# Query blocks filled ahead of the small steps, turned values copied by two engines, keys times beta formed ahead of the decays

## The reference, cut to what matters

```
x = x + 1/2 * RMSNorm(SwiGLU_1(RMSNorm(x)))
x = x + RMSNorm(Mix(RMSNorm(x)))
x = x + 1/2 * RMSNorm(SwiGLU_2(RMSNorm(x)))
```

```
# sample attention: scores of the new token's queries with all cached keys
s = einsum('bqhd,bkhd->bhqk', q, k) / 8 + cq - ck
# delta rule over the prompt, in chunks of 64 tokens
gc    = cumsum(g);  decay = exp(gc_i - gc_j) below the diagonal
kb    = k * beta
lower = (kb @ k.T) * decay;   attn = (q @ k.T) * decay
rhs   = [v * beta, kb * exp(gc)];  k_left = k * exp(g_last - gc)
```

## Time and profile before

| | |
|---|---|
| median of 3 runs | 1599.41 us (1598.86 to 1602.84) |
| profiled execution, its own time | 1597.58 us |
| its span, first to last instruction | 1595.3 us |
| PE busy | 1506.3 us, 94% of the span |
| DVE busy | 627.2 us, 39% |
| ACT busy | 500.7 us, 31% |
| POOL busy | 224.2 us, 14% |
| mean granted clock | 0.975 |
| DMA | 268.77 MB, mean 168 GB/s |

### The profile page before, as it was taken

How to read it: one execution, slowest core, us unless ns; L and a number is a source line. 1 busy time by engine, 2 the same in 40 slices (tenths; PEclk the granted TensorE clock), 3 DMA queues, 4 the chain that set the end, 5 groups by cost and what they waited for, 6 DMA issues and landing times. The chain is left out here.

```text
span 1595.3 us, 31169 instructions
## 1 busy us (share of the span) xinstructions
PE 1506.3 (94%) x12556; PEld 1382.2 (87%) x12556; DVE 627.2 (39%) x929; ACT 500.7 (31%) x740; POOL 224.2 (14%) x204
## 2 busy tenths in 40 slices
PE   7999999999688999999988999979979999999995
PEld 7999999999577888877866887759979999999995
DVE  4434343111633664133447443346253333432223
ACT  5322223211521355221124323242343222222221
POOL 0111111000252000323100220011031111110000
PEclk9999999999899999999989999989989999999998
DMA  4222222221449987999976757936212222223221
GB/s 151 92 92 92 92 92 99 92 90 62 146 149 387 340 299 249 366 336 341 377 260 217 238 186 259 300 116 227 80 40 90 86 89 90 92 97 109 81 83 53
DMA packets 111939, 268.77 MB, mean 168 GB/s; under 512 B 15401, under 2 KB 15914, under 8 KB 111090
## 3 DMA queue, kind: packets, MB, share of 16 engines
q1 hardware_dynamic: 105586, 244.25, 44.6%
q0 software_dynamic: 6272, 23.34, 4.0%
HBM read 253.29 MB, written 14.26 MB: 168 GB/s over the span
## 5 line engine op out<-in xcount | busy, mean ns | idle before, releaser
L131 DVE TENSOR_TENSOR w_low<-w_raw,w_high 128x1024 fp32r<-128x1024 f32 (+1 forms) x180 | 233.2, 1297 | 648.9 <-ACT w_high L127 648.8
L127 ACT ACTIVATE w_high<-w_raw 128x1024 fp32r<-128x1024 f32 (+1 forms) x180 | 200.7, 1116 | 731.6 <-PE psum L152 691.9
L148 PE MATMUL psum<-h_high,w_high 128*128 128x260 f32 x1344 | 270.5, 282 | 1.7 <-DVE w_low L131 1.7
L152 PE MATMUL psum<-h_high,w_low 128*128 128x260 f32 x1344 | 270.9, 283 | 0.0
L150 PE MATMUL psum<-h_low,w_high 128*128 128x260 f32 x1344 | 270.4, 283 | 0.0
L148 PEld LDWEIGHTS psum<-h_high,w_high 128*128 128x128 f32 x1344 | 207.2, 188 | 2.4 <-DVE w_low L131 2.4
L152 PEld LDWEIGHTS psum<-h_high,w_low 128*128 128x128 f32 x1344 | 207.2, 188 | 0.0
L150 PEld LDWEIGHTS psum<-h_low,w_high 128*128 128x128 f32 x1344 | 206.6, 188 | 0.0
L148 PE MATMUL psum<-mix_h_high,w_high 128*128 128x260 f32 x704 | 147.6, 291 | 6.3 <-DVE mix_h_low L296 6.1
L148 PE MATMUL psum<-a_high,w_high 128*128 128x260 f32 x704 | 144.2, 286 | 0.0
L150 PE MATMUL psum<-mix_h_low,w_high 128*128 128x260 f32 x704 | 142.5, 284 | 0.0
(11 more groups left out here) (324 smaller groups left out, 1921.3 us busy)
## 6 DMA issues: line engine op xcount, KB each, us to landing
kv_ring<-in_cache_k SPq DMA_DIRECT2D x256, 256.0 KB, 4.5
kv_ring<-in_cache_v SPq DMA_DIRECT2D x256, 256.0 KB, 4.4
w_raw<-in_w_gu SPq DMA_DIRECT2D x88, 512.0 KB, 3.2
w_raw<-in_w_dn SPq DMA_DIRECT2D x32, 704.0 KB, 4.0
w_raw<-in_w_proj SPq DMA_DIRECT2D x44, 512.0 KB, 6.7
spill<-h_f POOLq DMA_DIRECT2D x20, 260.0 KB, 5.2
gates<-spill POOLq DMA_DIRECT2D x16, 260.0 KB, 3.9
w_raw<-in_w_merge SPq DMA_DIRECT2D x8, 512.0 KB, 4.4
```

The source lines that it names most:

```text
L127: act.activation(w_high[:, u, 0:nk, :], w_raw[:, u, 0:nk, :], ACT.Copy).then_inc(high_done, 1)
L131: dve.tensor_tensor(w_low[:, u, 0:nk, :], w_raw[:, u, 0:nk, :], w_high[:, u, 0:nk, :].bitcast(F32), ALU.subtract).then_inc(low_done, 1)
L148: pe.matmul(out[h], w_high[:, u, k, :], high[:, k0 + j, tok[h]], start=s, stop=False)
L152: mm = pe.matmul(out[h], w_low[:, u, k, :], high[:, k0 + j, tok[h]], start=False, stop=e)
```

## The change

It has three parts; no arithmetic is added or taken out.

1. On DVE `queries(0)` moves from behind the small steps to ahead of them, behind a wait for `lin_out` (the copy of block 3 by ACT). `split_low` of block 6 moves from behind the scan to ahead of the reciprocal.
2. Of the four copies of turned values ACT does banks 0 and 1 (new semaphore `vt_first`), DVE banks 2 and 3. On DVE they now stand ahead of the low parts of g and beta. PE waits for both semaphores.
3. In `spread` DVE forms KB and v times beta first, with no wait but `p_bc`, and then waits for exp(g). The count of `p_dve` changes: KB is 1, v is 2, the difference is 3, KBE 4. In `raw` PE waits for count 2 alone ahead of k times KB, which now goes to bank 7 (beta's bank, read by then), and for the decays only ahead of k times q.

```diff
@@ scalar, before the attention loop
                     act.activation(gbr[64:68, 1, :], cum[64:68, :], ACT.Copy).then_inc(parts_high, 1)
+                    act.wait_ge(stored, 48)
+                    act.wait_ge(vt_pe, NQ)
+                    for b in range(NQ // 2):
+                        act.activation(vtok[:, b, :], psum[:, b, :], ACT.Copy).then_inc(vt_first, 1)
                     act.wait_ge(levels_in, 32)
@@ scalar, spread
-                            act.wait_ge(p_dve, 9 * i + 1)
+                            act.wait_ge(p_dve, 9 * i + 3)
                             act.activation(el[:, :], el[:, :], ACT.Exp).then_inc(p_act, 1)
@@ vector, small steps
                     split_low(dve, n0 + 5, 1, KD)
+                    dve.wait_ge(lin_out, Q0 + 4)
+                    queries(0)
                     dve.wait_ge(small_act, 5)
...
                     dve.tensor_scalar(rows[0:64, :], wsum[0:64, :], coef[0:64, 0:1], -1.0, ALU.mult,
                                       ALU.mult).then_inc(small_dve, 1)
+                    split_low(dve, n0 + 6, 0, KD)
                     dve.wait_ge(small_dve, 5)
                     dve.reciprocal(rows[64:96, :], wb[64:96, :]).then_inc(small_dve, 1)
...
-                    dve.wait_ge(lin_out, Q0 + 4)
-                    queries(0)
                     for n in range(4, NB):
-                        if n + 2 < NB:
+                        if 4 < n < NB - 2:
                             split_low(dve, n0 + 2 + n, n % 2, KD)
@@ vector, before the attention loop
                     queries_apart(0)
+                    dve.wait_ge(stored, 48)
+                    dve.wait_ge(vt_pe, NQ)
+                    for b in range(NQ // 2, NQ):
+                        dve.tensor_copy(vtok[:, b, :], psum[:, b, :]).then_inc(vt_copy, 1)
                     dve.wait_ge(parts_high, 1)
...
-                    dve.wait_ge(stored, 48)
-                    dve.wait_ge(vt_pe, NQ)
-                    for b in range(NQ):
-                        dve.tensor_copy(vtok[:, b, :], psum[:, b, :]).then_inc(vt_copy, 1)
@@ vector, spread
+                            dve.tensor_tensor(tmp[:, KB, :], k, psum[:, 7, :], ALU.mult).then_inc(p_dve, 1)
+                            dve.tensor_tensor(v, v, psum[:, 7, :], ALU.mult).then_inc(p_dve, 1)
                             dve.wait_ge(p_act, 3 * i + 1)
+                            dve.tensor_copy(gl[:, :], gb[:, :, C - 1]).then_inc(p_last, 1)
                             dve.tensor_copy(egl[:, i, :], ...).then_inc(p_last, 1)
-                            dve.tensor_copy(gl[:, :], gb[:, :, C - 1]).then_inc(p_last, 1)
-                            dve.wait_ge(p_last, 2 * i + 2)
+                            dve.wait_ge(p_last, 2 * i + 1)
                             dve.tensor_tensor(el[:, :]..., gb, ALU.subtract).then_inc(p_dve, 1)
-                            dve.tensor_tensor(v, v, psum[:, 7, :], ALU.mult).then_inc(p_dve, 1)
-                            dve.tensor_tensor(tmp[:, KB, :], k, psum[:, 7, :], ALU.mult).then_inc(p_dve, 1)
-                            dve.wait_ge(p_dve, 9 * i + 3)
+                            dve.wait_ge(p_dve, 9 * i + 1)
                             dve.tensor_tensor(tmp[:, KBE, :], tmp[:, KB, :], eg[:, :], ALU.mult).then_inc(p_dve, 1)
@@ vector, raw
-                            dve.tensor_tensor(lt[:, i, :], psum[:, 5, :], tmp[:, DT, :], ALU.mult).then_inc(p_dve, 1)
+                            dve.tensor_tensor(lt[:, i, :], psum[:, 7, :], tmp[:, DT, :], ALU.mult).then_inc(p_dve, 1)
@@ tensor (twice: key_pair with r, and after the transposes)
-                    pe.wait_ge(vt_copy, NQ)
+                    pe.wait_ge(vt_first, NQ // 2)
+                    pe.wait_ge(vt_copy, NQ // 2)
@@ tensor, raw
-                            pe.wait_ge(p_dve, 9 * i + 3)
-                            pe.wait_ge(p_act, 3 * i + 2)
+                            pe.wait_ge(p_dve, 9 * i + 2)
                             k = cv[:, 4 + i, 0:SEQ]
                             for p in range(NQ):
-                                pe.matmul(pr(psum[:, 5, :], p), pr(k, p), pr(tmp[:, KB, :], p), start=True, stop=True)
+                                pe.matmul(pr(psum[:, 7, :], p), pr(k, p), pr(tmp[:, KB, :], p), start=True, stop=True)
+                            pe.wait_ge(p_act, 3 * i + 2)
                             for p in range(NQ):
                                 mm = pe.matmul(pr(psum[:, 6, :], p), pr(k, p), pr(cv[:, i, 0:SEQ], p), start=True, stop=True)
```

More of the change, by code:

```diff
@@ L670, in core @@
             vt_copy = sem("fox_values_copied")
+            vt_first = sem("fox_first_values_copied")
             fs_pe = sem("fox_scores")
@@ L1271, in _ @@
                     split_low(dve, n0 + 5, 1, KD)
-                    dve.wait_ge(small_act, 5)
-                    dve.scalar_tensor_tensor(out=wsum[:, :], in0=wz[:, :], scalar=0.0, in1=wl[:, :],
-                                             op0=ALU.max, op1=ALU.add).then_inc(small_dve, 1)
-                    dve.tensor_scalar(wb[64:96, :], wb[64:96, :], 1.0, None, ALU.add).then_inc(small_dve, 1)
-                    dve.wait_ge(small_dve, 4)
-                    dve.tensor_scalar(rows[0:64, :], wsum[0:64, :], coef[0:64, 0:1], -1.0, ALU.mult,
-                                      ALU.mult).then_inc(small_dve, 1)
-                    dve.wait_ge(small_dve, 5)
-                    dve.reciprocal(rows[64:96, :], wb[64:96, :]).then_inc(small_dve, 1)
-                    dve.wait_ge(small_dve, 7)
-                    dve.tensor_tensor_scan(cum[:, :], starts[:, :], rows[:, 0:SEQ], 0.0, ALU.mult,
-                                           ALU.add).then_inc(small_dve, 1)
                     def queries(r):
@@ L1295, in queries @@
                                                 ).then_inc(qbd_done, 1)
+                    dve.wait_ge(lin_out, Q0 + 4)
+                    queries(0)
+                    dve.wait_ge(small_act, 5)
+                    dve.scalar_tensor_tensor(out=wsum[:, :], in0=wz[:, :], scalar=0.0, in1=wl[:, :],
+                                             op0=ALU.max, op1=ALU.add).then_inc(small_dve, 1)
+                    dve.tensor_scalar(wb[64:96, :], wb[64:96, :], 1.0, None, ALU.add).then_inc(small_dve, 1)
+                    dve.wait_ge(small_dve, 4)
+                    dve.tensor_scalar(rows[0:64, :], wsum[0:64, :], coef[0:64, 0:1], -1.0, ALU.mult,
+                                      ALU.mult).then_inc(small_dve, 1)
+                    split_low(dve, n0 + 6, 0, KD)
+                    dve.wait_ge(small_dve, 5)
+                    dve.reciprocal(rows[64:96, :], wb[64:96, :]).then_inc(small_dve, 1)
+                    dve.wait_ge(small_dve, 7)
+                    dve.tensor_tensor_scan(cum[:, :], starts[:, :], rows[:, 0:SEQ], 0.0, ALU.mult,
+                                           ALU.add).then_inc(small_dve, 1)
                     def new_forgets():
```

## The result

The change takes the median from 1601.07 us (1597.81 to 1603.62, six runs) to 1583.80 (1580.31 to 1584.70, six runs): a ratio of 0.9889, 95% interval [0.9874, 0.9904], 17.3 us. The forecast was 1582.0. The profiled execution took 1584.02.

A forecast was written before the change was run, and what follows sets the result against it. PE, busy for 94% of the span, was taken as the bound, so time could come only from its idle or low-clock places. 8.6 + 2.5 + 4.7 + 1.5 = 17.3 us gave 1582 against the median, range 1578 to 1588.

The forecast's parts named there:

- The queries: Between block 4 and the first key pair: PE's 6.98 us wait and 1.59 of low clock go, 8.6 us together.
- The turned values: Before the first scores: copies on ACT and DVE side by side let PE resume 2.5 us earlier.
- KB first: At `raw` of the four heads: PE's waits for KB shrink, 4.7 us in sum, ends 4 to 5.4.
- what is late next: At `turn` 2: PE still waits for DVE's list, so 1.0 of head 2's 1.5 us was counted.
- The clock: Three low-clock stretches from 818 to 861 us: 1.5 us gained net, ends 3.6 and -1.5.
- the second stretch: Low clock from 824 to 831 us, priced at some 1.4 us: should go.
- the first may: Low clock from 818 to 824 us, priced at some 2.7 us: may go, half counted.
- the third likely stays: Low clock from 854 to 861 us, priced at some 2.8 us: likely stays in some form.
- transfers did not eat part 1: Rival, key waits between 480 and 600 us: they grow from 6.1 to 12.2, gain 11.2, time 1588; chance 0.06.
- the copies were held by the gathers: Rival at the queries: one copy passes per gather, the pair starts as before, gain 8.7, time 1591; chance 0.03.
- the clock was not low for long: Rival: clock at 0.50 from 816 to 867 us, 12 us slower, time 1611; chance 0.02.

The follow-up runs named there:

- before_again: The kernel before the change, with no edit, run and profiled a second time on the first chip: 1601.0 us (one run).
- Part 1 alone: Kernel before plus only the early query copies and the early `split_low` of block 6: 1590.07 us, ratio to before 0.9937.
- part 2 alone: Kernel before plus only the turned-value copies shared by ACT and DVE, ahead of the low parts: 1597.30 us, ratio to before 0.9970.
- part 3 alone: Kernel before plus only KB and v formed first, PE waiting for these alone, KB's product into bank 7: 1596.10 us, ratio to before 0.9972.
- q_last: Changed kernel, with DVE's product of q with its decay moved behind the attention matrix: 1573.98 us, ratio to before 0.9863.
- after_again: Changed kernel with no edit, profiled once on the second chip: 1574.87 us (one run).
- bank0_first: Changed kernel, but PE starts the scores after ACT's first copy and waits for the other banks later: 1575.56 us, ratio to before 0.9883.
- ring_late: Changed kernel, with the third and fourth slot of the first keys loaded later, behind two more weight blocks: 1575.85 us, ratio to before 0.9886.
- after_timed: Changed kernel with no edit, timed on the third chip: 1577.01 us, ratio to before 0.9885.
- split_late: Changed kernel, with `split_low` of block 6 back at its old place behind the scan: 1576.89 us, ratio to before 0.9882.

## Why the prediction was right, point by point

The stages by lead, second profile of before less the changed kernel's, both with the stretch of single matmuls (start times in us):

| place | before_again | changed | lead | gained since the row above |
|---|---|---|---|---|
| first key pair | 476.08 | 467.30 | 8.8 | 8.8 |
| second key pair | 485.31 | 475.12 | 10.2 | 1.4 |
| last pair of the projection | 816.62 | 806.50 | 10.1 | -0.1 |
| first scores | 825.69 | 813.12 | 12.6 | 2.5 |
| `raw` 0 | 834.55 | 819.79 | 14.8 | 2.2 |
| `raw` 2 | 858.63 | 840.91 | 17.7 | 3.0 |
| pair behind `raw` 3 | 873.31 | 854.77 | 18.5 | 0.8 |
| `merge` | 1072.75 | 1055.61 | 17.1 | -1.4 |

*The queries: right.* Predicted 8.6, the wait and the low clock behind it; measured 10.2 to the second pair, of which 7.1 are the wait and 1.4 the pair; the other 1.7 lay ahead of the wait, 0.4 before the stretch of single matmuls and 1.3 in its length, and are no part of the change. Part 1 alone shows 8.5. The new wait for `lin_out` cost nothing. Four more points of that step held: the copies come at once behind block 5, block 6 is in time, transfers move with PE (waits for keys 6.4 where 6.3 stood), and the gathers don't hold the copies up but for 0.16 us. On the last, the Trainium skill ("SBUF — State Buffer", "SBUF: two separate sides") would have had DVE's copies locked out while POOL works. The eight took 1.68 us beside gathers in all ten kernels with part 1, against 1.52 clear of them; what is more is one copy that ends with its gather (0.31 instead of 0.16), and before_again's 1.61, which also overlap a gather, have such a copy of 0.26. What the prediction left out is the other direction: gathers that begin inside `split_low` are held (below, on the hardware). They are not on PE's path, and the median of the 64 is as before (0.946, before 0.947).

*The turned values: right.* Predicted 2.5, measured 2.45 of wait; what part 2 alone gave beyond it is under the clock. The two engines did not hinder each other in PSUM: ACT's two copies took 1.08 and DVE's two 1.29, side by side.

*KB first: right in sum, with one thing missed.* Predicted 4.7. From `spread` 0 to the pair behind `raw` 3 it is 37.56 us in the changed kernel (817.21 to 854.77) and 43.00 in before_again (830.31 to 873.31): 5.4 us; less the new wait for keys, 1.3, it is 4.1. In part 3 alone the same way is 5.2 shorter and the wait 0.7, which leaves 4.5, and it timed 4.5. (The table has 6.0 from the first scores on; 0.5 of it lies ahead of `spread` 0.) The missed thing is that wait. The list of "what is late next" stopped at `turn`, and didn't follow the ring. A pair uses two of the ring's four slots, so the pair two places on needs the slots that this one frees. The refill took until 12.66 us after the start of the pair that freed them (849.09 to 861.75). In the kernel before PE took 12.53 us for the same way (863.02 to 875.55) and met no wait; without the wait of `raw` 3 (0.96 to 0.98) it needs 11.36 of work. In the ten profiles with part 3 the way was 11.96 to 12.91 us, 12.3 in the mean, and in the four without it 12.51 to 12.53, so of the 1.2 us taken out some 0.2 are kept. The DMA share falls to 0.06 from 845 to 852 and is 0.95 from 852 to 861: the transfers wait for the slots, not the other way round, until then. And as q_last showed, of what is gained ahead of the pair that frees the slots the ring takes little: the wait for keys grew by 0.1 only. What is gained between the two pairs is what goes.

*The clock: near in size, partly by luck.* The prediction took 1.5 us net, from "the second stretch should go, the first may, the third likely stays". The first stayed in five of the seven profiles with a wait of 1.81 us and was gone in two. From the start of the transposes to `spread` 0 these seven took 6.21 to 7.87 us, 7.2 in the mean; the four with the old wait of 4.26 took 10.85 three times and 10.17 once, 10.7 in the mean. That is 3.5 us, 1.0 more than the wait of 2.45, and the 1.0 is clock.

The second and third stood in one of the four profiles with the old waits at the heads, where they cost 4.0 us (46.95 from `spread` 0 to the pair behind `raw` 3, the other three 42.84 to 43.05): 1.0 in the mean. The third came back in two of the eight profiles with 1.95 us at `turn` 2 (after_again, bank0_first), 1.6 us each: 0.4 in the mean.

An estimate from these means is 1.0 + 1.0 - 0.4 = 1.6. So the runs don't contradict the 1.5, but with so few profiles they don't show it either, and it was worked out from one trace whose second and third stretch are the exception. Without the term the gain would have been forecast as 15.8 us, the time as 1583.6 (measured 1583.8, but from a median of before that lay 1.7 us above the one forecast from). What the waits' lengths say of the clock is less than the prediction took from them (next section but one).

The end: 8.6 + 2.5 + 4.7 = 15.8 us without the clock term, beside 17.3 measured; the interval of the ratio, times 1601.07, is 15.4 to 20.2 us and holds both 15.8 and the forecast 17.3. Of the table's 17.1 at `merge`, 1.7 lay ahead of the change, which leaves 15.4 between these two profiles.

The rivals: transfers did not eat part 1 (part 1 alone: 10.1 us), the copies were held by the gathers for 0.16 us only, and the clock was not low for long (0.85 from 815 to 822, then 1.00; in after_again one stretch at `turn` 2).

## What to carry to other kernels

When a wait goes, follow the path past every resource that PE's own progress releases, not only past the next engine in the list: here a ring of buffers that PE came back to after 12.5 us, and that needed 12.0 to 12.9, became the next bound as soon as 1.2 us were taken out between its two uses. Price the clock only from several executions of the same kernel; a low stretch behind a short wait in one trace is no evidence that removing the wait pays for it. And a second profile of the unchanged kernel costs little: without it, 5.7 us lost at another place, in a stretch that the unchanged kernel has too, would have been charged to the change.

## What the runs showed of the hardware

*The same wait, with and without the fall of the clock.* Behind 1.81 us of idle at the scores the pair of 32 matmuls took 3.60, 3.41, 3.40, 3.52 and 2.77 us in five profiles (changed kernel, part 2 alone, ring_late, after_timed, q_last) and 1.93 in two (after_again, split_late). Behind 2.34 us at head 0, the product took 2.08 once and 1.16 in three others. Behind 0.75 it was 1.93 both times, behind 4.26 always over 3.4. Behind 1.95 us at `turn` 2 the clock fell in two of eight. So idle times of some 2 us are followed by the lower clock in some executions and not in others, at the same place of the same program.

*PE's matmuls one at a time.* In five profiles (the changed kernel's first, before_again and the three parts) PE was busy for about half of the stretch from 443 to 449, with gaps of 0.4 to 0.9 us that no semaphore explains; in the first profile of before and in all eight of the second and third chip there were none. From 440 to 443 the DMA share was 0.96 to 1.06 with the gaps, and 0.49 to 1.06 without. They cost 5.7 to 7.5 us. The instruction queue's transfer before it (16 KB, queue q8) starts 18.2 to 18.3 us after the projection's first matmul and takes 1.03 to 1.05 us with the gaps, and 18.0 to 18.2 and 1.03 to 1.05 in seven of the nine profiles without, so no late transfer of instructions is seen; the cause stays open.

*A gather that begins inside DVE's `split_low` is held.* In the 14 profiles 79 gathers began 0.14 to 0.75 us inside one. All 79 took 1.30 to 1.90 us instead of 0.94, and ended 0.81 to 0.82 us after it. The `split_low` reads two inputs from SBUF; beside the reciprocal, with one input, 31 gathers all took 0.94 to 0.95. The `split_low` that began in a running gather wasn't longer for it (1.23 at 440.10 in before, 0.71 us into a gather). Nothing on PE's path waited for a gather here.

*Chips differ more than many edits do*: the kernel before took 1592.6 to 1601.0 us in the median on three chips, 8.4 us or 0.5%, while the changed kernel's ratio was 0.9885 and 0.9889. All four profiles on the first of the three chips have the single matmuls, none of the eight on the others has them; they may be most of the difference, which no run here shows.
